# Three norm boundaries, context columns first: a change to a three-layer transformer kernel on one core

## The reference

```python
a = rms_norm(h) * (1 + scale) + shift          # mean of squares over the 1024 features, per token
h = h + gate * sublayer(a @ w_in ...) @ w_out
...
def rms_norm(x, w=None):
    y = x * lax.rsqrt(jnp.mean(x * x, axis=-1, keepdims=True) + EPS)
```

## Time and profile before

| | us |
|---|---|
| timed runs | 1502.47, 1506.96, 1507.47 (median 1506.96) |
| the profiled execution | span 1503.5 (the page gives no other time of it) |
| PE busy | 1422.7 (95%) |
| DVE, ACT, POOL busy | 818.4, 666.7, 835.4 |
| mean granted clock of PE | 0.971 |

### The profile page before, as it was taken

How to read it: one execution, slowest core, us unless ns; L and a number is a source line. 1 busy time by engine, 2 the same in 40 slices (tenths; PEclk the granted TensorE clock), 3 DMA queues, 4 the chain that set the end, 5 groups by cost and what they waited for, 6 DMA issues and landing times.

```text
span 1503.5 us, 22602 instructions
## 1 busy us (share of the span) xinstructions
PE 1422.7 (95%) x8800; PEld 1215.9 (81%) x8800; DVE 818.4 (54%) x1554; ACT 666.7 (44%) x1076; POOL 835.4 (56%) x665
## 2 busy tenths in 40 slices
PE   6989999999999999877999999999999999999997
PEld 3868888999988887544778888888878865999997
DVE  3787677786676697677675333321126667322211
ACT  3436764445452233674442322232226376544442
POOL 0533417998965443664435454554446630699985
PEclk9999999999999999977999999999999999999999
DMA  9656605777775642000445555543333320355563
GB/s 368 258 181 254 231 18 208 254 251 245 241 254 201 216 161 96 15 29 1 143 151 195 196 185 195 187 140 90 103 104 108 112 89 1 114 195 185 182 188 119
DMA packets 71322, 242.98 MB, mean 162 GB/s; under 512 B 7472, under 2 KB 13104, under 8 KB 70832
## 3 DMA queue, kind: packets, MB, share of 16 engines
q1 hardware_dynamic: 68800, 237.15, 46.5%
q10 hardware_dynamic: 2416, 4.39, 1.0%
HBM read 239.42 MB, written 1.05 MB: 160 GB/s over the span
## 4 chain that ended last, share of the span: by engine, by line
PE 51%; DVE 3%; ACT 2%; POOL 1%; issue 1%; DMA 0%; DVEq 0%; ACTq 0%
PE bank L539 15%; PE bank L540 14%; PE bank L541 14%; PE cond_a L960 1%; PE bank L960 1%; PE bank L676 1%; PE cond_a L1020 1%; PE bank L677 1%; PE bank L968 1%; PE bank L680 1%; PE bank L980 1%; PE cond_b L980 0%; PE cond_b L968 0%; ACT w_hi L1278 0%; DVE scratch L2572 0%
## 5 line engine op out<-in xcount | busy, mean ns | idle before, releaser
L1783 POOL TENSOR_TENSOR w_lo<-raw,w_hi 128x512 fp32r<-128x512 f32 (+1 forms) x612 | 774.0, 1291 | 629.9 <-ACT w_hi L1278 618.0
L1278 ACT ACTIVATE w_hi<-raw 128x1024 fp32r<-128x1024 f32 (+3 forms) x301 | 308.9, 1029 | 601.3 <-PE bank L541 522.5
L539 PE MATMUL bank<-h_hi,w_hi 128*128 128x256 f32 (+2 forms) x1604 | 525.6, 328 | 5.6 <-DVE h_lo L1842 2.6
L541 PE MATMUL bank<-h_hi,w_lo 128*128 128x256 f32 (+2 forms) x1604 | 522.3, 326 | 0.0
L540 PE MATMUL bank<-h_lo,w_hi 128*128 128x256 f32 (+2 forms) x1604 | 522.1, 326 | 0.0
L539 PEld LDWEIGHTS bank<-h_hi,w_hi 128*128 128x128 f32 (+1 forms) x1604 | 302.5, 189 | 38.1 <-DVE h_lo L1842 5.8
L541 PEld LDWEIGHTS bank<-h_hi,w_lo 128*128 128x128 f32 (+1 forms) x1604 | 302.3, 188 | 26.3
L540 PEld LDWEIGHTS bank<-h_lo,w_hi 128*128 128x128 f32 (+1 forms) x1604 | 302.6, 189 | 25.8
L539 PE MATMUL bank<-hidden_hi,w_hi 128*128 128x256 f32 (+1 forms) x528 | 167.6, 317 | 0.5 <-POOL w_lo L1783 0.5
L540 PE MATMUL bank<-hidden_lo,w_hi 128*128 128x256 f32 (+1 forms) x528 | 167.3, 317 | 0.0
L541 PE MATMUL bank<-hidden_hi,w_lo 128*128 128x256 f32 (+1 forms) x528 | 167.3, 317 | 0.0
(11 more groups left out here) (420 smaller groups left out, 1790.7 us busy)
## 6 DMA issues: line engine op xcount, KB each, us to landing
raw<-in_up SPq DMA_DIRECT2D x132, 512.0 KB, 3.5
ada_w<-in_ada SPq DMA_DIRECT2D x128, 512.0 KB, 4.5
raw<-in_down SPq DMA_DIRECT2D x48, 448.0 KB, 3.4
raw<-in_out SPq DMA_DIRECT2D x24, 512.0 KB, 3.5
raw<-in_down SPq DMA_DIRECT2D x24, 512.0 KB, 3.6
raw<-in_in SPq DMA_DIRECT2D x24, 512.0 KB, 3.6
arena<-in_ada SPq DMA_DIRECT2D x16, 512.0 KB, 11.8
raw<-in_uq SPq DMA_DIRECT2D x12, 384.0 KB, 3.0
```

The lines of the kernel that those rows point to most:

```text
L539: pe.matmul(out, w_h, x_h, start=first, stop=False)
L541: return pe.matmul(out, w_l, x_h, start=False, stop=last)
L1278: act.activation(part_slot(w_hi, f, u), raw_slot(f, u), ACT.Copy).then_inc(s["rounded"], 1)
L1783: pool.tensor_tensor(part_slot(w_lo, f, u)[:, a:b], raw_slot(f, u)[:, a:b], part_slot(w_hi, f, u)[:, a:b].bitcast(F32), ALU.subtract).then ...
```

## The change

At the three boundaries the work is cut into context columns (0 to 255) and latent columns (256 to 511).

- **End of the old phase** (`ctx_then_lat`): the last three units (out1), or the last product (down1), run over the context columns first, all three with their weights held, then over the latent ones. The context norm's sums and spread stand in PE's list between matmuls of the latent pass. For down0, where the context tokens do not depend on it, sums and spread stand after units 8 and 11 (`context_norm`).
- **Start of the new phase** (`lat_after_ctx`): the first three units run over the context columns; the latent norm's sums and spread stand between them; then the latent columns follow. The `early` path is kept only where latent tokens alone are normed.
- **DVE and ACT** get lists to match (`staged_residual`, `joint_residual`; `ctx_square`, `ctx_std`, `shift_ctx`, `lat_square`), with new semaphores.

The core of the diff:

```diff
+            def ctx_sums(tail):
+                chains[0] += 1
+                pe.wait_ge(s["sums_in"], chains[0])
+                for i in range(2):
+                    last = pe.matmul(bank[5][:, i:i + 1], sq_sum[:, i * P:(i + 1) * P], ones[:, 0:1], ...)
+                if tail:
+                    pe.wait_ge(s["ctx_sq"], tail)
+                    ...
+                last.then_inc(s["sum_ready"], 1)
+            def spread_ctx():
+                pe.wait_ge(s["inverse_ready"], chains[0])
+                ...
+            def ctx_then_lat(name, K=KD, hi=h_hi, lo=h_lo):
+                f = ph[name]
+                units = range(f.units - SLOTS, f.units)
+                ...
+                for u in units:
+                    ...
+                    for n, k in enumerate(of[u]):
+                        ...
+                        last = side(f, u, k, slice(0, L0), K, hi, lo, ahead)
+                    if u % f.parts == f.parts - 1:
+                        last.then_inc(s["ctx_steps"], 1)
+                        ctx_tiles[0] += 1
+                for j, u in enumerate(units):
+                    if not ahead:
+                        pe.wait_ge(s["ctx_res"], before + j + 1)
+                    for n, k in enumerate(of[u]):
+                        if (j, n) == (0, 4):
+                            ctx_sums(ctx_tiles[0])
+                        if (j, n) == (1, 2):
+                            spread_ctx()
+                        last = side(f, u, k, slice(L0, L1), K, hi, lo)
+                    last.then_inc(s["steps"], 1)
+            def lat_after_ctx(name, sums, spread, by_unit=False):
+                ...
+                pairs = [(u, k) for u in range(SLOTS) for k in range(KD)] if by_unit else \
+                    [(u, k) for k in range(KD) for u in range(2)] + [(2, k) for k in range(KD)]
+                before = {(0, 6): sums, (1, 4): spread} if by_unit else {(0, 3): sums, (0, 6): spread}
+                for u, k in pairs:
+                    if (u, k) in before:
+                        pe.wait_ge(s["h_work"], ctx_end)
+                        before[u, k]()
+                    ...
+                    if u == 0:
+                        ctx_gate(k)
+                    side(f, u, k, slice(0, L0))
+                for k in range(KD // 2):
+                    lat_gate(k)
+                    for u in range(SLOTS):
+                        side(f, u, k, lat)
+                for u in range(SLOTS):
+                    for k in range(KD // 2, KD):
+                        ...
+                    last.then_inc(s["steps"], 1)
+            def context_norm(u):
+                if u == 8:
+                    ctx_sums(0)
+                if u == 11:
+                    spread_ctx()
...
-            linear("in1", 0, TOK, gate=next_h(), after=spread_last, early=True)
+            lat_after_ctx("in1", lambda: token_sums(L0, L1, joint=True),
+                          lambda: spread_inverse(L0, L1, lat=4), True)
+            linear("in1", 0, TOK, first=SLOTS, after=spread_last)
...
+                phase(name, job, stop_at=KD - SLOTS)
+                for k in range(KD - SLOTS, KD):
+                    ctx_square(k)
+                ctx_std()
+                round_next()
+                lat_square(f, KD - 3)
+                shift_ctx(1, 1, 0, 2)
+                round_next()
+                lat_square(f, KD - 2)
+                shift_ctx(1, 1, 2, KD)
+                lat_square(f, KD - 1)
+                rms_std(L0, L1)
...
+            def joint_residual(name, chunk, prepare):
+                for k in range(KD):
+                    ...
+                    if k == KD - 1:
+                        lower(KD - 2)
+                        lower(KD - 1)
+                        carried(f, 3 * k)
+                    product_in(f, 3 * k + 2)
+                    joined(name, chunk, k, L0, L1, 0, L0).then_inc(s["taken"], 1)
+                    if k == 1:
+                        for q in range(1, 4):
+                            context_sums(q)
+                    if k == 2:
+                        for q in range(4, KD):
+                            context_sums(q)
+                        dve.nop().then_inc(s["sums_in"], 1)
+                    if k == 3:
+                        invert_ctx()
+                    ...
+            def staged_residual(name, chunk, n, which, split, prepare, third):
+                ...
+                if split < KD - 1:
+                    right(KD - 3)
+                invert_ctx()
+                scaled(0)
+                scaled(1)
+                lower(0)
+                scaled(2)
+                lower(1)
+                if split < KD - 1:
+                    right(KD - 2)
+                    add_square(KD - 3, L0, L1)
+                scaled(3)
+                lower(2)
+                for k in range(4, KD):
+                    scaled(k)
+                    if k < KD - 1:
+                        lower(k - 1)
+                if split < KD - 1:
+                    add_square(KD - 2, L0, L1)
+                else:
+                    dve.nop().then_inc(s["sums_in"], 1)
+                right(KD - 1)
+                lower(KD - 2)
+                round_third(third)
+                lower(KD - 1)
```

More of the change, by code:

```diff
@@ L579, in spread_inverse @@
                 last.then_inc(s["inverse_spread"], 1)
+            def ctx_sums(tail):
+                chains[0] += 1
+                pe.wait_ge(s["sums_in"], chains[0])
+                for i in range(2):
+                    last = pe.matmul(bank[5][:, i:i + 1], sq_sum[:, i * P:(i + 1) * P], ones[:, 0:1],
+                                     start=(i == 0), stop=(not tail and i == 1))
+                if tail:
+                    pe.wait_ge(s["ctx_sq"], tail)
+                    for i in range(2):
+                        last = pe.matmul(bank[5][:, i:i + 1], work[:, 1, i * P:(i + 1) * P], ones[:, 0:1],
+                                         start=False, stop=(i == 1))
+                last.then_inc(s["sum_ready"], 1)
+            def spread_ctx():
+                pe.wait_ge(s["inverse_ready"], chains[0])
+                for i in range(2):
+                    last = pe.matmul(bank[5][:, i * P:(i + 1) * P], inverse[:, i:i + 1].to_broadcast([P, P]),
+                                     ident, start=True, stop=True)
+                last.then_inc(s["inverse_spread"], 1)
             def feature_sums(t0, t1):
-                token_sums(t0, t1, halves=t0 < L0 and norms[0] > 0)
+                token_sums(t0, t1)
                 spread_inverse(t0, t1)
@@ L693, in linear @@
                         last.then_inc(s["steps"], 1)
-                for u in range(first, f.units):
+                for u in range(first, stop or f.units):
                     pe.wait_ge(s["split"], 2 * (f.first_unit + u) + (1 if M == P else 2))
@@ L1335, in round_h, with shift_h @@
                 h_count[0] += KD
-            def shift_h(n, which, both):
+            def shift_h(n, which, both, lat=late):
                 for k in range(KD):
@@ L1341, in shift_h @@
                     for a, b, m in ([(0, L0, 1)] if both else []) + [(L0, L1, 0)]:
[L1342 removed]
+                        last = act.activation(h_hi[:, k, slice(a, b) if both else lat], scaled_at(n, k)[:, a:b], ACT.Identity,
                                               bias=mod[:, n % 2, 24 * which + k, m:m + 1])
@@ L1973, in lower @@
                     for a, b, m in sides:
-                        own = slice(a, b) if both else late
-                        last = dve.scalar_tensor_tensor(out=h_lo[:, k, own], in0=scaled_at(n, k)[:, a:b],
-                                                        scalar=mod[:, n % 2, 24 * which + k, m:m + 1],
-                                                        in1=h_hi[:, k, own].bitcast(F32),
-                                                        op0=ALU.add, op1=ALU.subtract)
+                        last = lower_side(n, which, k, slice(a, b) if both else own, m, scaled_at(n, k)[:, a:b])
                     last.then_inc(s["h_split"], 1)
@@ L2404, in ffn0 @@
                 hidden_low(0, KF - 1, L0, L1)
-                residual("down0", 5, False, True, joint_gain)
+                joint_residual("down0", 5, joint_gain)
             def swiglu(n, both):
                 t0 = 0 if both else L0
-                norm(1, both, third=f"up{n}")
                 f = ph[f"up{n}"]
@@ L2418, in swiglu @@
                 hidden_low(n, KF - 1, t0, L1)
-                residual(f"down{n}", 5, both, prepare=(lambda: next_gain(2)) if n == 1 else None)
             def mixer1():
```

331 lines of the change are left out of this document (233 added, 98 removed).

## The result

The changed kernel takes 1517.0 us (median of 10 runs, 1507.8 to 1520.2) against 1504.7 of the kernel before, timed beside it (10 runs): ratio 1.0073, 95% interval 1.0055 to 1.0090. By the ratio that is 11 us slower (the two medians lie 12.3 apart), outside the range given. The kernel is slower, and the likeliest case ("the same") was wrong.

The account below looks back on a forecast made before the run. TensorE, busy 95% of a 1503.5 us span, was taken as the bound. Boundary terms of +1.2, -1.4 and -2.0 us gave -2.2, put on the 1506.96 us median: 1504.8 us, range 1498 to 1510.5.

Parts of the forecast that it names:

- the same: Whole kernel: a time not told from no change, which needs about 0.3%, 4.5 us; chance 0.57.
- Context chain of A: In down0: PE waits 2.6 us for the context sums after unit 8 and 0.9 us after unit 11.
- A: Boundary from down0 to in1: 8.6 us forecast for 7.42, so 1.2 us slower.
- Latent sums of A: Six context tiles after down0's end: PE waits 0 to 0.3 us, or 1.9 if weights come late; 0.3 taken.
- B: Boundary from out1 to up1: 7.05 us forecast for 8.46, so 1.4 us faster.
- C: Boundary from down1 to ckv: 5.3 us forecast for 7.31, so 2.0 us faster.
- Context chains of B and C: Under the latent pass of the old phase: PE waits about 0.25 us in B, nothing in C.
- Latent sums of B and C: 2.1 us after the old phase's last unit: PE waits 1.1 us in B and 0.75 in C.
- What is late next: Before the new phase's unit 3: PE waits 1.2 us in B, 0.65 in A, 0.1 in C.
- the clock falls where it did not: Rival: clock drops to 1.2 GHz at four new waits beside one-column sums, 8.2 us slower, 1515; chance 0.12.
- All cover holds: Rival: DVE and ACT keep ahead, none of the forecast's 7.85 us of waits is left, 1496.9 us; chance 0.22.
- The weights fall behind: Rival: ACT and POOL start late at all three phase starts, 2.2 us slower, 1509; chance 0.11.

Follow-up runs that it names:

- e8: Kernel before with only boundary C staggered and its scaled context columns in SBUF instead of PSUM; ratio 1.0014 to the kernel before.
- e10: e7 with boundary A put back as in the kernel before; ratio 0.9984 to the kernel before (1503.4 us).
- e7: Changed kernel with A's context sums later, its inverse and carried product earlier, latent sums of B and C later, Silu table early; 0.9960 to kernel before, 1500.5 us.
- e12: e7 with 20 matmuls ahead of TensorE's 2.44 us wait at 76 us of the span; ratio 0.9982 to the kernel before.
- e9: e7 without the ScalarE activation that asks early for the Silu table; ratio 0.9968 to the kernel before.
- e5: Changed kernel with 24 and 20 filler matmuls in TensorE's two long waits at A; ratio 1.0035 to the kernel before.
- e11: Kernel before with 20 matmuls ahead of TensorE's 2.44 us wait at 76 us of the span; ratio 1.0018 to the kernel before.

## Why the prediction was wrong, step by step

**Context chain of A.** Forecast: 2.6 us after unit 8 and 0.9 after unit 11; measured 3.01 and 0.65, together 3.66 for 3.5. This step, which I trusted least, was right in mechanism and size.

**Latent sums of A.** This is the first step that failed: "PE waits 0 to 0.3 ... I take 0.3" became 2.60. The queue on VectorE was read rightly (low parts, carried product, last add), but not its durations. Its rows in the changed kernel:

```profile
441.13 2.69 DVE L2114 SCALAR_TENSOR_TENSOR h_lo<-scratch,mod,h_hi 128x256 fp32r<-128x256 f32 x2 [0.17 <-DVE std L2498]
443.75 1.21 DVE L2016 CUSTOM_DVE_ANT_0 ada_junk<-ada_w,cond_a 128x1024 bf16<-128x1024 f32 x1
...
446.02 0.47 DVE L2535 SCALAR_TENSOR_TENSOR X<-bank,mod,X 128x256 f32<-128x256 f32 x1
```

Two low parts take 2.69 us where I had 0.40 each: 1.9 of the 2.3 us that were missing. GpSimd works beside both of them:

```profile
437.93 5.61 POOL L1935 TENSOR_TENSOR w_lo<-raw,w_hi 128x512 fp32r<-128x512 f32 x4
```

I took the price from instructions with one operand in PSUM. The low parts of the kernel before, with both tensors in SBUF, take 0.40 too, but beside an idle GpSimd:

```profile
762.28 0.87 DVE L1975 SCALAR_TENSOR_TENSOR h_lo<-work,mod,h_hi 128x256 fp32r<-128x256 f32 x2
```

The trace before did show the other price, in a row that I did not read. VectorE's additions in down0, all in SBUF, by tile (count, then ns minimum/median/maximum):

```profile
L2311 DVE TENSOR_TENSOR std<-std,work x6: 661/796/1357, 387.7 to 429.7; 128x256 f32<-128x256 f32 x6
```

Beside them stand, additions of the same size with a PSUM operand, at 0.43. GpSimd is at work for 37.3 of the 41.7 us from 388.0 to 429.7. That the low parts of A and B are stretched for the reason found in e8 is argued from these rows; the place of the operand was changed only at C.

**Context chains of B and C.** Forecast 0.25 and 0; measured 0.29 and 0.

**Latent sums of B and C.** Forecast 1.1 us in B; measured 2.26 + 0.35 = 2.6. Here too two low parts were stretched, while GpSimd worked on the new phase's weights:

```profile
758.66 1.61 DVE L2114 SCALAR_TENSOR_TENSOR h_lo<-work,mod,h_hi 128x256 fp32r<-128x256 f32 x1 [0.19 <-ACT h_hi L1441]
...
762.34 1.44 DVE L2114 SCALAR_TENSOR_TENSOR h_lo<-work,mod,h_hi 128x256 fp32r<-128x256 f32 x1 [0.16 <-ACT h_hi L1441]
```

```profile
757.44 2.55 POOL L1935 TENSOR_TENSOR w_lo<-raw,w_hi 128x512 fp32r<-128x512 f32 x2 [10.40 <-ACT w_hi L1390]
760.95 2.55 POOL L1935 TENSOR_TENSOR w_lo<-raw,w_hi 128x512 fp32r<-128x512 f32 x2 [0.96 <-ACT w_hi L1390]
```

That is 1.21 + 1.04 = 2.25 us more than 0.40 each; PE waited 1.5 us longer than forecast. In C, with its scaled columns in PSUM, 0.17 + 0.23 = 0.4 us was measured for 0.75. On PE, C went from 38.6 us (1102.69 to 1141.28) to 36.6 (1114.76 to 1151.33), from the start of down1's last tile to the fourth unit of the new phase: the 2.0 that were forecast. Some 0.6 of it is given back at the next wait, 1.76 us for ckv's low part and not 1.19.

**What is late next.** 1.2 us before unit 3 of up1: measured 1.12. 0.65 before unit 3 of in1: 0.47. 0.1 in C: none.

**The clock.** This is the second step that failed, and the larger one. The sum takes the slow clock of the old boundaries away, 0.11 x 15.6 + 0.21 x 16.6 + 0.11 x 15.5 = 6.9 us, and puts nothing behind the new waits ("a granted clock of 1.00 there"); some 6.6 us of it came back at other places. The timed executions agree: their mean granted clock is 0.971 before (101 executions in the three comparisons) and 0.973 changed (10), where 6.9 us less would have made it 0.976. The rival "the clock falls where it did not" had 0.12, and its mechanism is what happened, at three places and not four. I set a bare wait of 2.44 us followed by 1.00 against it. That was one draw of one execution. The same wait with the same code behind it was followed, from 76.5 to 80 us, by 1.00 in three profiles (before, e8, e10) and by 0.51 to 0.75 in the other nine that leave it unfilled. The place of a wait matters more than I had it. The waits of 2.0 to 3.0 us at A and B, which stand beside the one-column sums, were followed by 1.2 GHz every time they were left unfilled, 11 of 11 in six profiles; the wait for ckv's low part, 1.66 to 2.16 us in the eleven kernels that stagger C, in three of eleven (e7, e8, e12). So the likeness that I set aside, to the boundaries, was the right one, and that to the wait of 2.44 us the wrong one; why they differ is not shown. The row of the changed kernel at that wait:

```profile
76.50:80.00 3.50, 3.50 (x17) 3.50 (x18) 3.43 (x4) 0.01 (x1) 1.75 (x2) 0.52 0.18 75
```

The cost of the slow clock by the windows shown above is 4.9 us at A and 2.6 x 0.50 + 4 x 0.09 = 1.7 at B. With it the sum closes: forecast +1.2 - 1.4 - 2.0 = -2.2; waits beyond the forecast, A 0.4 - 0.25 + 2.3 - 0.2 = 2.3 and B 1.5; given back behind C 0.6; clock 6.6; together 8.8 us, against 8.7 measured in the three stretches. The single boundaries close less well: A 8.4 for 7.2, B 1.8 for 2.8. That the total meets within 0.1 us is partly luck, as A alone scatters by 2.4 us from one profile to the next.

**The other rivals.** The clock rival's own figure, 1515 us, lies nearest to the 1517.0 measured, though it counted four falls and left the forecast's waits as they were. "All cover holds" failed at both A and B. "The weights fall behind" did not happen in the changed kernel: PE waits there for w_lo only 0.47 us at in1.

## What to carry to other kernels

A wait that a restructuring adds is not priced at its own length: where it stands beside light work, as the one-column sums here, add what the half clock behind it may cost (4.9 us for waits of 5.6 at A, 1.7 for 2.26 at B; the shortest wait with a fall behind it in a staggered boundary was 1.52 us), and take "no fall seen" from several executions and from a place of the same kind. Before a chain is laid under another engine's work, price each of its instructions from rows in which that work runs beside it and the operands lie in the same memory. When sums are laid under matmuls, put their place in the list by the time at which the slower chain is done: moving two insertion points, one inverse and one carried product (e9) turned 11 us of loss into some 5 us of gain.

## What the runs showed of the hardware that I had not expected

- A VectorE operation with two SBUF tensors (128x256) takes 0.47 us alone and 1.1 to 1.6 us while GpSimd runs on SBUF tensors; with one tensor in PSUM, 0.47 to 0.48 either way. GpSimd's pair of instructions goes from 2.55 to 2.73 us in e8.
- After the same wait of some 2.4 us TensorE's clock is 1.00 in some executions and 0.51 to 0.75 in others. Shorter waits are no safe ground: 1.60 us in e8 was followed by 0.58, and 1.52 us in e9 by 0.50 from 441 us on, while 1.12 us was followed by 1.00, and so was one of 2.16 us (e9, ckv's low part, 1160.5 to 1168).
- Twenty or more otherwise useless matmuls in a wait hold the clock: 4.5 us gained at A in e5, nothing in e11.
